# A decoder block in two parts on one core: picks moved between query columns and ahead of a wait, and the input loaded first

## The chip, the cores and the metric

One core of a Trainium2 chip runs one program. The metric is the device time of one execution in microseconds, as the median of several. The engines are TensorE (PE; its weight loads are PEld), VectorE (DVE), ScalarE (ACT), GpSimd (POOL) and SyncE (SP); DMA engines move data between HBM and the on-chip memory, issued by SP and by POOL.

## What is computed

The reference runs two blocks over one sequence of 256 tokens of 1024 numbers, in float32. The first block has two layers of band attention with a short convolution and a gated feed-forward. The second has two layers too; layer 0 has an mLSTM mixer, layer 1 stick-breaking attention over shared keys and values, and both end in an expert layer ("PEER"), cut here:

```python
def peer_ffn(h, w_q, sub_keys, peer_u, peer_v):
    def block(xb):                                    # 128 tokens
        q = einsum('td,de->te', xb, w_q).reshape(128, 8, 2, 128)
        s = einsum('thpk,pnk->thpn', q, sub_keys)     # 2 x 128 scores for each of 8 heads
        s_top, i_top = top_k(s, 16)
        ...                                           # 16 best of the 256 sums of both sides
        u = take(peer_u, expert, axis=0)              # 8 x 16 rows of 1024 for each token
        act = gelu(einsum('thkd,td->thk', u, xb))
        vv = take(peer_v, expert, axis=0)
        return einsum('thk,thkd->td', softmax(g_top) * act, vv)
```

The condition vector c passes a SiLU and a matrix product to give the shifts, scales and gates of the second block. In layer 1 of the second block q and k are normed by head before the scores.

## The kernel before, in words

The 256 tokens are two tiles of 128, with a token in each partition. An expert layer has 8 x 16 = 128 **picks** for each tile. Pick q is, for each of the tile's 128 tokens, one row of 2 x 1024 numbers (u and v of one expert) that an indirect DMA from POOL fetches into one of 10 places (`ROW`, rings `ring_b`, two slots of `wring`, `ring_c`). In the stretch from pick 248 of the whole program to pick 353 two of the 10, `ring_c`, are lent to weights, so there are 8. There are four tiles of picks: two of layer 0, then two of layer 1. The picks of one tile are worked off while the next tile's dense work runs, under one schedule written out by hand.

Each pick takes four steps. POOL (L1915) issues it once PE has released its place (`rows_free`), and, for the first of some heads, once the indices are there (`chosen`). DVE (L2672) takes the dot product of the u half with the token's row. ACT (L1709, L1713, L1719) makes gelu, weight and a diagonal matrix, for two picks at a time. PE (L1269, `weighted`) multiplies that by the v half and adds it up, two picks at a time (a pair).

How far each engine is to have come with the picks at a step of the dense work stands in `plan_of(t)` (L151): a list of step names and counts that `counted` sums up. `picks(tt, k)` on DVE does the dots up to k, `gelus(tt, k)` on ACT likewise, `weighted(tt, k)` on PE does the products up to the last whole pair before k, and with `False` up to k itself. All engines run their lists in order, so a product that isn't ready blocks what is written behind it.

`second_layer(t)` (one on each engine) is the dense work of layer 1 for tile t, with the picks of tile tt = 1 + t between its steps: norm, six weight slots ("in") for keys, values and queries, `heads_normed` of the key rows and then of the query rows on DVE (L2738), their transposes on PE (L1027, "heads"), the scores, logarithms, sums and exponents of the attention ("core", 4 groups of heads for t = 0, 8 for t = 1), output product ("o", "mid", "out"), norm ("fnorm", "fcols"), then four query column groups (`late_queries`, L1387) each followed by scores against the keys (`late_keys`, L1140), and last `choose`, the top-16 and index work on DVE, whose `choose` plan spreads picks over its own steps. `choose` of heads 0 to 3 waits for the second bank of key scores. Weights of the second layer come by SP, each into a slot that `used2` on PE returns.

At the begin SP loads the condition row `crow` (512 KB, one row to all partitions), the two halves of the input `x` (512 KB each), the 64 KB identity, small parameters and then the weights of 2 MB each, in that order (L530 on). ACT takes the SiLU of `crow` (L1434) and then the squares of `x` (L1424). PE waits for the identity, runs 28 matmul records on it (`idle_products`, L740) and then transposes the scaled input (L721). POOL waits for the first weights, loads three constants, waits for the SiLU and then loads the rows of the condition's matrix.

## Time and profile before

| | us |
|---|---|
| median of 3 runs | 2526.04 (2524.95 to 2527.66) |
| the profiled execution | 2526.39, its span 2524.7 |
| PE busy | 2032.2 (80%) |
| PE weight loads | 1384.9 (55%) |
| DVE busy | 1719.8 (68%) |
| ACT busy | 955.0 (38%) |
| POOL busy | 658.8 (26%) |
| DMA | 823.98 MB, mean 326 GB/s; indirect queue 595.97 MB |

The profile is of one execution. The page gives the busy time of each engine, the span in 40 slices (63.1 us each) and the costliest groups of instructions; the other views are the timeline (instructions in order, with the idle time before each and what ended it), the windows (busy times, clock and DMA rate of a stretch), the waits, and the DMA issues with their time to landing. A fp32 matmul has two records in it, so a pair of picks is 8 records of L1269. A product's line says "x8" for one pair. The chain of work that ended last is put down to PE by 47%, to DMA by 27% and to DVE by 11% of the span.

### The profile page before, as it was taken

The page shows a single profiled execution, that of the slowest core. Times are in us where ns is not written, and L with a number is a line of the kernel's source. Part 1 is how long each engine was busy: PE and PEld are TensorE (multiplying, and loading weights), DVE is VectorE, ACT ScalarE, POOL GpSimd, SP SyncE. Part 2 cuts the span into 40 slices and gives each one's busy share as a digit, 9 for nine tenths or more (in the row PEclk, how much of TensorE's full clock was granted, in tenths as well). Part 3 has the DMA queues.
Part 4 walks back from the last instruction along what each step waited for, and adds up shares of the span by engine and source line. Part 5 has one row for each costly group of instructions (what it writes and reads, how often), then busy time and mean ns, then how long its engine had stood idle before and what let it go on. Part 6 is the DMA issues. An engine that isn't in the chain of part 4 may idle for free.

```text
span 2524.7 us, 33890 instructions
## 1 busy us (share of the span) xinstructions
PE 2032.2 (80%) x12150; PEld 1384.9 (55%) x12150; DVE 1719.8 (68%) x3454; ACT 955.0 (38%) x2101; POOL 658.8 (26%) x631
## 2 busy tenths in 40 slices
PE   8999999999999999997665587777577778556555
PEld 7999899899989979874321123243122325211111
DVE  5687787768778867677588555558754757776544
ACT  4434533444544345432332224423223732322222
POOL 0000001000000100024445433344432335444442
PEclk9999999999999999999887798899788889887767
DMA  7545577674547763279999999999999999999998
GB/s 304 212 167 209 182 277 283 240 262 161 202 172 277 268 256 142 84 319 388 422 421 422 419 423 422 403 421 421 412 404 401 421 410 383 421 422 421 422 421 337
DMA packets 110947, 823.98 MB, mean 326 GB/s; under 512 B 14432, under 2 KB 15344, under 8 KB 31040
## 3 DMA queue, kind: packets, MB, share of 16 engines
q0 software_dynamic: 90000, 595.97, 57.8%
q1 hardware_dynamic: 20784, 225.89, 23.3%
q8 instruction: 96, 1.57, 0.2%
q14 instruction: 67, 0.55, 0.1%
HBM read 820.76 MB, written 1.05 MB: 326 GB/s over the span
## 4 chain that ended last, share of the span: by engine, by line
PE 47%; DMA 27%; DVE 11%; ACT 5%; issue 4%; POOL 2%; DVEq 2%; ACTq 1%; SPq 0%; POOLq 0%
DMA ring_b<-in_peer_uv,eidx 17%; PE pd L647 14%; PE pa L647 10%; PE pr L1269 9%; PE pr L647 7%; DMA wring<-in_peer_uv,eidx 6%; DVE wring_r L1971 2%; DVE ring_b L2672 2%; DMA ring_c<-in_peer_uv,eidx 1%; DVE wring L2672 1%; PE pa L1387 1%; ACT junk L1719 1%; POOL ring_b L1915 1%; PE pd L1292 1%; PE pa L1292 1%
## 5 line engine op out<-in xcount | busy, mean ns | idle before, releaser
L1269 PE MATMUL pr<-ring_b,junk 128*64 128x512 f32 x880 | 288.6, 765 | 156.5 <-ACT junk L1719 155.8
L1269 PE MATMUL pr<-wring,junk 128*64 128x512 f32 x840 | 269.4, 748 | 171.1 <-ACT junk L1719 170.6
L1915 POOL DMA_INDIRECT ring_b<-in_peer_uv,eidx x220 | 252.9, 1150 | 532.8 <-PE pr L1269 302.4
L2672 DVE CUSTOM_DVE_ANT_0 ring_b<-ring_b,hrow 128x1024 f32<-128x1024 f32 x220 | 267.9, 1224 | 180.9 <-DMA ring_b<-in_peer_uv,eidx 174.2
L2672 DVE CUSTOM_DVE_ANT_0 wring<-wring,hrow 128x1024 f32<-128x1024 f32 x210 | 255.4, 1223 | 187.8 <-DMA wring<-in_peer_uv,eidx 181.7
L1915 POOL DMA_INDIRECT wring<-in_peer_uv,eidx x210 | 247.8, 1180 | 332.6 <-PE pr L1269 277.3
L1709 ACT ACTIVATE gel<-dots 128x2 f32<-128x2 f32 x255 | 51.8, 203 | 654.4 <-DVE dots L2672 650.7
L1899 POOL DMA_DIRECT2D aring<-in_ada_rows x112 | 60.2, 538 | 840.9 <-DVE adal L2066 787.3
L1269 PEld LDWEIGHTS pr<-ring_b,junk 128*64 128x64 f32 x880 | 69.3, 165 | 350.8 <-ACT junk L1719 242.6
L1269 PEld LDWEIGHTS pr<-wring,junk 128*64 128x64 f32 x840 | 64.1, 159 | 345.6 <-ACT junk L1719 243.5
L1971 DVE TENSOR_TENSOR wring_r<-wring,wtop 128x2048 fp32r<-128x2048 f32 x76 | 171.7, 2261 | 54.7 <-ACT wtop L1431 52.4
L647 PE MATMUL pd<-hhi,wring_r 128*128 128x256 f32 x960 | 204.2, 281 | 0.0
L1971 DVE TENSOR_TENSOR wring_r<-wring,wring_r 128x2048 fp32r<-128x2048 f32 (+1 forms) x77 | 173.7, 2262 | 38.1 <-ACT wring_r L1431 35.7
L1431 ACT CAST wring_r<-wring 128x2048 fp32r<-128x2048 f32 x80 | 149.7, 1886 | 70.0 <-DMA wring<-in_w_mix 25.1
L1431 ACT CAST wtop<-wring 128x2048 fp32r<-128x2048 f32 x80 | 149.1, 1882 | 62.7 <-DMA wring<-in_w_back 24.4
L1269 PE MATMUL pr<-ring_c,junk 128*64 128x512 f32 x328 | 109.1, 754 | 75.1 <-ACT junk L1719 74.7
L647 PE MATMUL pa<-flo_b,wring_r 128*128 128x256 f32 x768 | 166.6, 283 | 0.0
L647 PEld LDWEIGHTS pd<-hhi,wring_r 128*128 128x128 f32 x960 | 158.6, 188 | 0.1
L1719 ACT ACTIVATE junk<-halves,gel 128x64 f32<-128x64 f32 x510 | 149.6, 340 | 17.8 <-issue 0.3
L2066 DVE CUSTOM_DVE_ANT_0 aring<-aring,crow 128x1024 f32<-128x1024 f32 x112 | 136.5, 1218 | 13.9 <-DMA aring<-in_ada_rows 12.6
L2672 DVE CUSTOM_DVE_ANT_0 ring_c<-ring_c,hrow 128x1024 f32<-128x1024 f32 x82 | 100.0, 1223 | 55.4 <-DMA ring_c<-in_peer_uv,eidx 53.5
L1713 ACT ACTIVATE gel<-gel,wexp 128x1 f32<-128x1 f32 x510 | 122.7, 287 | 18.8 <-issue 1.4
(441 smaller groups left out, 4566.4 us busy)
## 6 DMA issues: line engine op xcount, KB each, us to landing
wring<-in_w_mix SPq DMA_DIRECT2D x38, 2048.0 KB, 8.8
aring<-in_ada_rows POOLq DMA_DIRECT2D x112, 512.0 KB, 5.1
wring<-in_w_ffn SPq DMA_DIRECT2D x22, 2048.0 KB, 8.3
wring<-in_w_lstm SPq DMA_DIRECT2D x12, 2048.0 KB, 7.7
wring<-in_w_stick SPq DMA_DIRECT2D x12, 2048.0 KB, 11.7
wring<-in_w_back SPq DMA_DIRECT2D x8, 2048.0 KB, 8.1
ring_c<-in_w_stick SPq DMA_DIRECT2D x5, 2048.0 KB, 12.1
wring<-in_w_back SPq DMA_DIRECT2D x4, 1536.0 KB, 6.9
```

Of the source, the lines that this page charges most:

```text
L647: m = nc.tensor.matmul(out_, lhsT, rhs, start=start, stop=stop)
L1269: m = nc.tensor.matmul(pr[half][side, :], diag[:, p % DIAGS, :], row(p)[:, D + half * 512:D + (half + 1) * 512], start=p in FIRST_OF_SIDE, ...
L1292: i = nc.tensor.matmul(b[:, :], src(k), w(k), start=(k == 0), stop=(k == KC - 1))
L1431: nc.scalar.copy(hi, raw).then_inc(whi_ready, 1)
L1709: nc.scalar.activation(gel[:, p:p + PART], dots[:, p:p + PART], ACT.Gelu)
L1713: nc.scalar.activation(gel[:, i:i + 1], gel[:, i:i + 1], ACT.Copy, scale=wexp[:, g * PART // PICKS % NT, c // TOPK, c % TOPK:c % TOPK + 1])
L1719: nc.scalar.activation(diag[:, q % DIAGS, :], halves[:, :], ACT.Copy, scale=gel[:, q % PICKS:q % PICKS + 1]).then_inc(diag_ready, 1)
L1899: pool.dma_start(aring[:, a, :], ins["ada_rows"][bass.ds(2 * i + a, 1)].rearrange("a p n -> p (a n)")).then_inc(ada_in[a], 16)
L1915: pool.indirect_dma_start(out=row(q), out_offset=None, in_=ins["peer_uv"], in_offset=bass.IndirectOffsetOnAxis(ap=eidx[:, tt % NT, CHOSEN[ ...
L1971: nc.vector.tensor_tensor(lo, raw, hi, ALU.subtract).then_inc(wlo_ready, 1)
L2066: nc.vector.tensor_tensor_reduce(out=aring[:, j % 2, :], in0=aring[:, j % 2, :], in1=crow[:, :], scale=1.0, scalar=0.0, op0=ALU.mult, op1= ...
L2672: m = nc.vector.tensor_tensor_reduce(out=row(q)[:, 0:D], in0=row(q)[:, 0:D], in1=hrow[:, q // PICKS % NT, SIDE[q], :], scale=1.0, scalar=0 ...
```

## The change

At the begin the two loads of `x` go ahead of that of `crow` on SP, and ACT's SiLU of `crow` goes behind the squares of `x`.

In layer 1 of the second block the plan has 4 picks instead of 3 (t = 0) or 2 (t = 1) for each of the first two late query groups, 2 instead of 4 (t = 0) or 2 (t = 1) for "keys", and for t = 1 20 instead of 23 over the choice of heads. So the counts are for t = 0: "q" 74 and 78 (before 73 and 76), "keys" 80 as before; for t = 1: "q" 92 and 96 (before 90 and 92), "keys" 98 (before 94), end of the choice 118 (before 117). In the first two late query groups PE now multiplies up to two picks short of "q" after the second of the four columns, and up to "q" itself behind the group; ACT does the matching gelus ahead of its copy of the group.

DVE does the dots up to "heads" (pick 31) ahead of its wait for the query rows and their norm, where it did them up to 29 and the other two behind the norm. PE does the products up to "heads" between the transposes of the key rows and those of the query rows, and ACT does the gelus for them behind its copies of the key columns.

```diff
@@ -150,10 +150,10 @@
 
 def plan_of(t):
 
-    out, q, step = ((3, 3, 48), (2, 2, 23))[t]
+    out, q, step = ((3, 4, 48), (2, 4, 20))[t]
     return counted(0, [("first", 2), ("norm", 2), ("cols", 4), ("col0", 2), ("col1", 2)] + [(("in", j), 3) for j in range(6)]
                    + [("heads", 2)] + groups_of(t) + [("o", 2), ("mid", 4 * t), ("out0", out), ("out1", out), ("fnorm", 2), ("fcols", 2), ("fcol0", 1), ("fcol1", 1)]
-                   + [(("q", j), q) for j in range(2)] + [("keys", 4 - 2 * t)] + choice("choose", step, 2 - t))
+                   + [(("q", j), q) for j in range(2)] + [("keys", 2)] + choice("choose", step, 2 - t))
 
 
 EARLY_COLUMNS = {(0, 2): (0, 0, 2, 4), (0, 3): (8, 10, 14, 16), (1, 2): (18, 20, 20, 24), (1, 1): (28, 30, 32, 34), (1, 3): (42, 44, 46, 48)}
@@ -527,9 +527,9 @@
 
         @block.sync
         def _(sp):
-            sp.dma_start(crow[:, :], ins["c_2"].partition_broadcast(P).rearrange("p a n -> p (a n)")).then_inc(c_in, 16)
             for t in range(NT):
                 sp.dma_start(x[:, t, :], ins["x"][0, t * P:(t + 1) * P, :]).then_inc(x_in, 16)
+            sp.dma_start(crow[:, :], ins["c_2"].partition_broadcast(P).rearrange("p a n -> p (a n)")).then_inc(c_in, 16)
             sp.dma_start(ident[:, :], ins["c_ident"]).then_inc(ident_in, 16)
 
             def load(l, i):
@@ -1307,9 +1307,9 @@
                     weighted(tt, at["in", j])
                 pe.wait_ge(sqk_ready, 2 * t + 1)
                 tile_columns(bank_a, pa_full, krow)
+                weighted(tt, at["heads"], False)
                 pe.wait_ge(sqk_ready, 2 * t + 2)
                 tile_columns(bank_a, pa_full, qrow)
-                weighted(tt, at["heads"])
                 pe.wait_ge(sT_ready, t + 1)
                 pe.wait_ge(stick_in, 96)
                 groups, g0, ks = STICK_GROUPS[t], STICK_BEFORE[t], t + 1
@@ -1396,8 +1396,8 @@
                     key_bank(lambda hp, cut: qpt[:, hp, cut], j)
 
                 for j in range(2):
-                    late_queries(j)
-                    weighted(tt, at["q", j])
+                    late_queries(j, lambda c: c == 1 and weighted(tt, at["q", j] - 2, False))
+                    weighted(tt, at["q", j], False)
                     late_keys(j)
                 weighted(tt, at["keys"])
                 for j in range(2, 4):
@@ -1429,9 +1429,6 @@
             def cast_half(n):
                 raw, hi = half_of(n, wring)
                 nc.scalar.copy(hi, raw).then_inc(whi_ready, 1)
-
-            act.wait_ge(c_in, 16)
-            nc.scalar.activation(crow[:, :], crow[:, :], ACT.Silu).then_inc(c_ready, 1)
 
             na = [0]
 
@@ -1477,6 +1474,8 @@
             nc.scalar.preload_act_table_set(ROOTS)
             for t in range(NT):
                 squares(0, t)
+            act.wait_ge(c_in, 16)
+            nc.scalar.activation(crow[:, :], crow[:, :], ACT.Silu).then_inc(c_ready, 1)
             upper(0, 0)
             tile_upper(0, 0, 0)
             upper(0, 1)
@@ -1812,8 +1811,8 @@
                 for dst in (skT[:, :, cut], sqT(t)):
                     for half in range(2):
                         nc.scalar.copy(dst[:, 4 * half:4 * half + 4, :], take().rearrange("p (c n) -> p c n", n=P)).then_inc(pa_free, 1)
+                    gelus(tt, at["heads"])
                 act.drain().then_inc(sT_ready, 1)
-                gelus(tt, at["heads"])
                 groups, g0 = STICK_GROUPS[t], STICK_BEFORE[t]
 
                 def logs(i):
@@ -1859,6 +1858,7 @@
                     act.drain().then_inc(sc_ready, 1)
 
                 for j in range(2):
+                    gelus(tt, at["q", j] - 2)
                     late_query(j)
                     gelus(tt, at["q", j])
                     late_key(j)
@@ -2744,10 +2744,9 @@
                 dve.wait_ge(stick_in, 96)
                 dve.wait_ge(srow_ready, 3 * t + 1)
                 heads_normed(krow, 0, 1.0)
-                picks(tt, at["in", 5])
+                picks(tt, at["heads"])
                 dve.wait_ge(srow_ready, 3 * t + 3)
                 heads_normed(qrow, 1, SB_DIM ** -0.5)
-                picks(tt, at["heads"])
 
                 groups, g0, ks = STICK_GROUPS[t], STICK_BEFORE[t], t + 1
 
```

## Rows read from the trace of the kernel before

**Rows 1.** The page, part 2: GB/s of the DMA engines in 40 slices
```profile
GB/s 304 212 167 209 182 277 283 240 262 161 202 172 277 268 256 142 84 319 388 422 421 422 419 423 422 403 421 421 412 404 401 421 410 383 421 422 421 422 421 337
```

**Rows 2.** Issue to landing of all picks' rows, from the view by tile
```profile
DMA to landing us min/median/max: 5.6/16.3/31.0
```

**Rows 3.** Timeline of the begin: start, duration (us), engine, line, idle before
```profile
8.11 5.89 PE L740 MATMUL pa<-ident 128*128 128x128 f32 x28 [8.11 <-DMA ident<-in_c_ident]
...
13.84 1.04 PE L721 MATMUL pd<-ident,hlo 128*128 128x128 f32 x8
```

**Rows 4.** Windows of 20 us: five engines' busy us, PEclk, DMA share, GB/s
```profile
1940.00:1960.00 20.00, 14.29 (x65) 5.70 (x65) 12.75 (x22) 14.48 (x32) 11.71 (x10) 0.89 0.93 357
...
2100.00:2120.00 20.00, 17.39 (x126) 11.56 (x124) 12.47 (x53) 6.07 (x22) 9.19 (x10) 1.00 0.76 304
```

**Rows 5.** Timeline of tile C's late queries, PE, POOL and DVE
```profile
2087.42 7.41 PE L1387 MATMUL pa<-hT,ring_c 128*128 128x128 f32 x64 [0.82 <-DVEq L2394]
...
2105.20 1.94 PE L1269 MATMUL pr<-wring,junk 128*64 128x512 f32 x8
...
2108.53 0.94 POOL L1915 DMA_INDIRECT wring<-in_peer_uv,eidx  x1 [8.37 <-issue]
...
2091.91 1.23 DVE L2672 CUSTOM_DVE_ANT_0 wring<-wring,hrow 128x1024 f32<-128x1024 f32 x1 [1.28 <-DMA wring<-in_peer_uv,eidx]
...
2108.70 1.65 DVE L2577 MAX8 top<-sc 128x8 f32<-128x128 f32 x8 [5.63 <-ACTq L1859]
...
2166.73 0.23 DVE L2654 TENSOR_TENSOR eidx<-hilof 128x64 int32<-128x64 f32 x1
...
2178.99 0.94 POOL L1915 DMA_INDIRECT ring_c<-in_peer_uv,eidx  x1 [0.31 <-issue]
```

**Rows 6.** Timeline of tile C's query rows, all engines
```profile
1910.90 1.55 POOL L1915 DMA_INDIRECT ring_b<-in_peer_uv,eidx  x1 [0.30 <-issue]
...
1926.82 1.22 DVE L2404 TENSOR_TENSOR cand<-sc 128x1024 f32<-128x1024 f32 x1
...
1935.02 1.97 PE L1027 MATMUL pa<-ident,sc 128*128 128x128 f32 x8 [10.18 <-DVEq L2738]
...
1936.92 2.70 PE L1269 MATMUL pr<-ring_b,junk 128*64 128x512 f32 x8
...
1937.02 0.58 ACT L1814 COPY hT<-pa 128x512 f32<-128x512 f32 x1 [0.27 <-PE pa L1027]
...
1939.55 1.71 PE L1325 MATMUL pd<-hT,skT 64*128 64x128 f32 x16
...
1945.51 5.24 PE L1269 MATMUL pr<-wring,junk 128*64 128x512 f32 x16 [2.38 <-ACT junk L1719]
...
1949.84 0.94 POOL L1915 DMA_INDIRECT wring<-in_peer_uv,eidx  x1 [2.94 <-PE pr L1269]
```

**Rows 7.** DMA issues, us to landing: tile C's pick 31, then 68
```profile
ring_b<-in_peer_uv,eidx POOLq DMA_INDIRECT x1, 22.8
...
ring_b<-in_peer_uv,eidx POOLq DMA_INDIRECT x1, 6.7
```

**Rows 8.** Waits of DVE in tile C's core, 1960 to 2028 (us, times, longest)
```profile
DVE sc L2773 <- PE pr L1338: 15.4, 7, 3.2
...
DVE wring L2672 <- DMA wring<-in_peer_uv,eidx: 0.3, 1, 0.3
```

**Rows 9.** Waits of DVE in tile B's core, 1575 to 1616
```profile
DVE wring L2672 <- DMA wring<-in_peer_uv,eidx: 5.0, 4, 1.3
```

**Rows 10.** Timeline of tile B's query rows, POOL and DVE
```profile
1520.68 0.93 POOL L1915 DMA_INDIRECT ring_c<-in_peer_uv,eidx  x1 [0.30 <-issue]
...
1540.49 1.22 DVE L2404 TENSOR_TENSOR cand<-sc 128x1024 f32<-128x1024 f32 x1
```

**Rows 11.** DMA issues, us to landing: tile B's pick 31, then 42
```profile
ring_c<-in_peer_uv,eidx POOLq DMA_INDIRECT x1, 28.5
...
wring<-in_peer_uv,eidx POOLq DMA_INDIRECT x1, 13.5
```

## The prediction

> **What bounds the kernel now.** I read the page first. Over the first 17 slices (to 1073 us) the DMA rate swings between 84 and 304 GB/s; from the 20th on it stands at 421 to 424 in most slices [rows 1]. That is the part in which the picks of the expert layers are fetched. A pick is one row of 8 KB for each of 128 tokens, 1.05 MB, so at 422 GB/s a pick costs 2.48 us, and what is left of the span is a count of megabytes plus the stretches in which the DMA engines had nothing to do. The change moves no byte, so after the first layers only those stretches count. The windows of 20 us show the two that matter here: 1940 to 1960 at 357 GB/s, which is (422 - 357) / 422 x 20 = 3.1 us lost, and 2100 to 2120 at 304, which is 5.6 us [rows 4]. A stretch is lost when all places of the ring are landed and not yet multiplied, so that POOL can't issue. The next question is therefore always the same: when does PE multiply pair (q, q+1), since POOL issues the pick 8 places on (10 in most stretches) right behind it. An issue needs at least 5.6 us to land; the median is 16.3 [rows 2], and the difference is what a late product may cost for nothing.
>
> I call the second layer's two token tiles B and C, and count picks from 0 in each.
>
> **The begin.** PE starts at 8.11, when the identity lands, and runs 28 products on it for 5.89 us; the first transpose of the input starts at 13.84, behind them [rows 3]. The identity is issued behind both the input and the condition row, in either order, so 8.11 stays. The input may land 1.2 us sooner (512 KB at 422 GB/s) and waits longer for PE. ACT's SiLU of the condition row moves behind the squares of the input, and GpSimd, which waits for it before its first weight rows, has a wait for the first weights ahead of that one. Price 0, bounds -0.3 and +0.3. The cover is the 5.89 us of products on the identity.
>
> **Tile C's query rows.** Before, DVE ends the dot of pick 29 at 1926.82 and at once norms the query rows, until 1935.02, when PE transposes them [rows 6]: 8.2 us. Now the dots of picks 30 and 31 come first. Pick 31 is issued at 1910.90 [rows 6] and lands 22.8 us later [rows 7], at 1933.7; the DMA engines are saturated until then, so it can't land sooner. Its dot ends at 1933.7 + 1.2 = 1934.9, the norm at 1943.1, so the query rows are 8.1 us later. That is an added wait: behind it on DVE stand the norm and the dots of 32 and 33, and PE, ACT and the whole core wait for the norm.
> What is gained: pair (28, 29) was multiplied at 1936.92, behind the transposes, and goes now right behind the key columns, at 1928, so picks 36 and 37 are issued 9 us sooner and the stall at 1940 goes. It also stood in the way of the first scores: ACT had the columns ready at 1937.02 + 0.58, PE began the scores at 1939.55 [rows 6]. So 8.1 - 1.9 = 6.2 us is the delay of the core; ACT's table loads and logarithms follow the scores at a fixed distance, and the products of 32 to 35, which began at 1945.51 and released the issue at 1949.84 [rows 6], move to 1951.7 and 1956.0.
> Pick 31 lands at 1933.7 and the queue is now never empty, so pick 39 lands 8 x 2.48 us later, at 1953.6. Pick 40 lands at 1956.0 + 5.6 = 1961.6. So the stall is not removed, it is moved 12 us on and is longer.
> Is it given back in the core? In tile C's core DVE waits 15.4 us for PE's sums and 0.3 us for rows [rows 8]: the chain scores, logarithms, sums, exponent, gelus sets the pace there and keeps a delay. The ring has 8 places here, and pick 68 landed 6.7 us after its issue [rows 7], 1.1 above the least. So of 6.2 us of delay 1.1 is free and 5.1 reach the DMA engines; since a restart leaves its second pick late too, I take +5.3. Bounds: +6.4 if nothing is free, and -3.1 if the core catches up and only the old stall goes. I take the upper part because the core's own waits [rows 8] are for PE, nearer to it than the landing waits that a catch-up needs.
>
> The Trainium skill (DMA: Bandwidth & Descriptors, Anatomy of one DMA) puts a transfer from GpSimd's queue at about 2.0 us plus its bytes at 436 GB/s, an estimate of 4.4 us for a lone pick. The trace has 5.6 as its least [rows 2], and it decides; by 4.4 the term would be 1.2 us less, +4.1.
>
> **Tile B's query rows.** The same step: pick 31 lands at 1520.68 + 28.5 = 1549.2, its dot ends at 1550.4, and the norm that began at 1540.49 [rows 10, 11] begins 9.9 us later; with 2 us given back as above the core is 7.9 us late. But there are 10 places here: pick 42, the first that waits for a core product, took 13.5 us to land [rows 11], 7.9 above the least. Just enough. And in this core DVE waits 5.0 us for rows on one ring alone [rows 9], so the delay shrinks by the core's end. I take +0.5, bounds 0 and +1.5.
>
> **The late queries.** In tile B the change only moves products inside the same ten picks; DVE does the dots up to pick 79 before its choice of heads, before and after, and the 27th slice (1641 to 1704 us) that holds the step stands at 421 GB/s [rows 1], with no stall to win: 0, bounds -0.5 and +0.5. In tile C the first 64 matmuls of a query column group start at 2087.42 and last 7.41 us; pair (88, 89) was multiplied at 2105.20, behind two groups, and POOL could issue pick 96 only at 2108.53 [rows 5]. That is the 5.6 us stall. Now pair (86, 87) goes at 2091 in the middle of the first group and (88, 89) behind it at 2094.7 (the dot of 89 begins at 2091.91 [rows 5] and ends 1.2 later, plus 1.5 us on ACT). Pick 96 is issued at 2097.4, pick 98 at 2101 (the place returns when the group is done, 5.4 us later than before, still early), 100 at 2105, 102 at 2112, 104 at 2119.5. With pick 89 landed at 2091.9 and 2.48 us for each, 104 must be issued by 2091.9 + 37.2 - 5.6 = 2123.5. The stall goes: -5.6.
> What is late next: five pairs instead of two lie ahead of the second key bank, and two waits for ACT, so the choice of heads, which began at 2108.70, begins at 2120.6. DVE has 20 picks to do in it instead of 23; from 2108.70 to the indices at 2166.73 [rows 5] it took 58.0 us, so at most 58.0 - 3 x 1.2 = 54.4 now, until 2175.0. Pick 0 of the next tile was issued at 2178.99 [rows 5] and lands by the median at 2195.3; with everything 5.6 us sooner it must be issued by 2195.3 - 5.6 - 5.6 = 2184. Covered by 9 us. But pick 98, landed at 2091.9 + 9 x 2.48 = 2114.2, gets its dot at 2122: DVE is 8 us behind the landings, and the margins of the issues shrink to a few us (104: 4). I add +0.5; bounds of the whole term -5.6 and -2.6.
>
> **Sum.** 0 + 0.5 + 5.3 - 5.6 + 0.5 = +0.7 us. The profiled execution took 2526.39 (span 2524.7 and 1.7 around it), 0.35 above the median of the runs, 2526.04; on the median the sum gives 2526.7, which I round to 2527.
>
> **Rivals.** (1) The query rows cost nothing: the core of tile C catches up and both stalls go, -3.1 - 5.6 + 0.5 + 0.5 = -7.7, 2518. For it: the delay starts with four more picks landed. Against it: DVE's waits in that core [rows 8]. It decides if the core's pair period is below two times 4 picks' landing, 19.8 us. Chance 0.24. (2) The late gain fails, slower: the choice of heads begins 12 us later and DVE, 8 us behind the landings, frees places too late, so that the stall at 2104 comes back inside the choice. It decides when the choice ends later than 2184, or an issue comes later than 5.6 us before its landing's turn. Price: the query term stays alone, +0.5 + 5.3 + 0.5, with 0.5 to 2 of new gaps: 2533. Chance 0.17. (3) The moves cancel nothing and do nothing, since all picks wait in the ring anyway: 2526. Against it: the two stalls of [rows 4] lie exactly on the moved steps. Chance 0.04. The forecast has 0.55.
>
> **How the numbers follow.** The forecast's own range is 2522.5 to 2531.5 (query term 3 to 6.4, late term -5.6 to -2.6, tile B 0 to 1.5). The whole range, 2517.5 to 2532, takes in rival 1 and stops short of most of rival 2. A measurement of this kernel can tell about 0.2% (5 us) from no change. Faster by that is rival 1 with a little of the forecast's edge, 0.25; slower is rival 2 with a little, 0.18; the rest, 0.57.
>
> **What would show it.** In the changed kernel's trace: the first 14 us as before; tile C's query transposes near 1943 (+ what tile B added) instead of 1935.02; a stall not at 1940 but near 1954 to 1960, and issue-to-landing times in tile C's core near 6; no stall at 2104, with products between the columns of each late group; the choice of heads starting near 2121. Wrong if the query transposes move by under 5 us, if the windows from 1940 to 2040 hold more than 415 GB/s on average, or if a new stall stands between 2120 and 2200.

## The result, and the profile after

| | median us (runs) | ratio to the kernel before | profiled execution |
|---|---|---|---|
| before | 2525.83 (6) | | 2526.39, span 2524.7 |
| after | 2536.95 (6) | 1.0046 [1.0033, 1.0059] | span 2534.8 |

The change costs 11 us. The forecast was 2527.0, range 2517.5 to 2532, with 0.57 on no change that can be told and 0.18 on slower: the measured time lies 5 us above the range. A ratio of 0.001 is 2.5 us here; below, each ratio is turned into us with 2526.

The DMA rates of the page after, to be held against [rows 1]: the 25th, 31st and 35th slice fell (422 to 390, 401 to 372, 422 to 371), and the 34th, with the old stall at 2104, rose (383 to 408). The view has one figure for each slice of 63 us.

```profile
GB/s 303 211 167 208 190 271 284 240 254 167 202 169 286 265 247 161 87 320 385 422 421 422 419 424 390 408 422 421 421 416 372 414 397 408 371 423 421 422 421 354
```

Windows of 20 us of the kernel after, with the columns of [rows 4]. The stall at 2100 is gone (304 to 422 GB/s). The one at 1940 is deeper (357 to 268), and there are new ones in tile B's core behind the query rows (1560), in tile C's choice (2140) and at its end (2180). The first fence has the kernel before for these three windows, the second the kernel after.

```profile
1560.00:1580.00 20.00, 16.93 (x56) 6.21 (x54) 14.66 (x25) 14.45 (x31) 10.32 (x9) 0.76 1.01 419
...
2140.00:2160.00 20.00, 11.71 (x80) 6.82 (x80) 16.97 (x43) 8.26 (x22) 9.68 (x8) 0.92 1.01 420
...
2180.00:2200.00 20.00, 10.57 (x32) 2.29 (x32) 10.86 (x18) 5.19 (x21) 9.03 (x8) 0.83 1.01 421
```

```profile
1560.00:1580.00 20.00, 14.09 (x54) 6.50 (x52) 12.01 (x22) 13.71 (x27) 4.41 (x6) 0.66 0.82 324
1940.00:1960.00 20.00, 12.56 (x52) 7.25 (x51) 12.01 (x21) 13.60 (x27) 4.82 (x5) 0.60 0.67 268
2100.00:2120.00 20.00, 15.98 (x107) 10.74 (x106) 9.86 (x16) 4.99 (x17) 9.82 (x9) 0.91 1.02 422
2140.00:2160.00 20.00, 14.72 (x108) 9.88 (x108) 19.49 (x76) 6.35 (x23) 12.15 (x8) 1.00 0.98 383
2180.00:2200.00 20.00, 14.71 (x96) 6.69 (x98) 11.51 (x22) 10.27 (x34) 6.15 (x6) 0.74 0.83 321
```

The timeline of tile C's query rows, answering to [rows 6]: DVE starts the norm at 1935.09 behind the dot of pick 31 (before 1926.82), PE transposes the query rows at 1943.30 (1935.02), begins the scores at 1945.98 (1939.55) and the core's first pairs at 1952.85 (1945.51). POOL, idle for 13.11 us, issues pick 40 at 1957.13 (1949.84).

```profile
1935.09 1.22 DVE L2404 TENSOR_TENSOR cand<-sc 128x1024 f32<-128x1024 f32 x1
...
1943.30 1.97 PE L1027 MATMUL pa<-ident,sc 128*128 128x128 f32 x8 [2.95 <-DVEq L2738]
1945.98 3.09 PE L1325 MATMUL pd<-hT,skT 64*128 64x128 f32 x16 [0.71 <-ACTq L1815]
1952.85 5.19 PE L1269 MATMUL pr<-wring,junk 128*64 128x512 f32 x16 [3.78 <-ACT junk L1718]
...
1957.13 0.94 POOL L1915 DMA_INDIRECT wring<-in_peer_uv,eidx  x1 [13.11 <-PE pr L1269]
```

The timeline of tile C's late queries and the end of its choice, answering to [rows 5], with ACT's lines (ACT's line numbers are one lower in the kernel after): products stand between the column halves (2100.24), pick 96 is issued at 2107.34, and then DVE sits idle for 9.07 us (before 5.63) until the second key bank, and starts the choice at 2131.47. At the end ACT waits 6.68, 4.60 and 5.70 us for PE's fourth query group, fourth key bank and the 64 matmuls of the rows, and POOL waits 7.12 and 5.82 us for products.

```profile
2100.24 1.94 PE L1269 MATMUL pr<-ring_b,junk 128*64 128x512 f32 x8
...
2107.34 0.94 POOL L1915 DMA_INDIRECT wring<-in_peer_uv,eidx  x1 [1.53 <-issue]
...
2131.47 0.68 DVE L2577 MAX8 top<-sc 128x8 f32<-128x128 f32 x3 [9.07 <-ACTq L1858]
...
2171.58 0.58 ACT L1853 COPY cand<-pa 128x512 f32<-128x512 f32 x1 [6.68 <-PE pa L1387]
2178.29 0.58 ACT L1857 COPY sc<-pa 128x512 f32<-128x512 f32 x1 [4.60 <-PE pa L1140]
2178.97 1.28 ACT L1682 ACT_TABLE_LOAD   x1
2180.26 0.26 ACT L1682 ACTIVATE wexp<-wexp 128x64 f32<-128x64 f32 x1
2190.23 0.58 ACT L1677 COPY hrow<-pa 128x512 f32<-128x512 f32 x1 [5.70 <-PE pa L1130]
...
2187.78 1.65 POOL L1915 DMA_INDIRECT ring_b<-in_peer_uv,eidx  x1 [7.12 <-PE pr L1269]
...
2199.26 1.22 POOL L1915 DMA_INDIRECT ring_c<-in_peer_uv,eidx  x1 [5.82 <-PE pr L1269]
```

Where the time went, by comparing the landing of the same pick in both traces (after less before): +0.7 when tile B begins, +3.5 at its pick 52, +1.5 at tile C's pick 34, +5.9 at 52, +8.1 at 84, +3.3 at 102, +11.7 at the next tile's pick 0, and +10.7 to +12.6 from there. So there are three steps: tile B's query rows, tile C's query rows, and a gain of 5 us between picks 84 and 102 that is more than given back before the tile ends.

### The profile page after: what moved, and what is told of

Same layout as the page of the kernel before. It is cut to its first block, busy times and chain, and to the rows that moved or that the text cites. A ratio compares the mean times of both kernels' runs of the same rounds, so it can differ in the third digit from the quotient of the medians.

```text
span 2534.8 us, 33890 instructions
## 1 busy us (share of the span) xinstructions
PE 2051.4 (81%) x12150; PEld 1393.1 (55%) x12150; DVE 1717.7 (68%) x3454; ACT 954.8 (38%) x2101; POOL 649.5 (26%) x631
## 4 chain that ended last, share of the span: by engine, by line
PE 48%; DMA 24%; DVE 13%; ACT 6%; issue 4%; POOL 2%; DVEq 2%; ACTq 1%; SPq 0%; POOLq 0%
PE pd L647 14%; DMA ring_b<-in_peer_uv,eidx 12%; PE pr L1269 10%; PE pa L647 10%; DMA wring<-in_peer_uv,eidx 7%; PE pr L647 5%; DMA ring_c<-in_peer_uv,eidx 3%; PE pa L1292 3%; DVE wring_r L1971 2%; DVE ring_b L2672 2%; DVE wring L2672 2%; ACT junk L1718 1%; PE pd L1292 1%; POOL ring_b L1915 1%; DMA aring<-in_ada_rows 1%
## 5 line engine op out<-in xcount | busy, mean ns | idle before, releaser
L1269 PE MATMUL pr<-wring,junk 128*64 128x512 f32 x840 | 274.6, 760 | 151.2 <-ACT junk L1718 150.9
L1915 POOL DMA_INDIRECT wring<-in_peer_uv,eidx x210 | 239.1, 1138 | 338.1 <-PE pr L1269 293.2
L1269 PE MATMUL pr<-ring_c,junk 128*64 128x512 f32 x328 | 121.5, 837 | 86.3 <-ACT junk L1718 86.2
L2066 DVE CUSTOM_DVE_ANT_0 aring<-aring,crow 128x1024 f32<-128x1024 f32 x112 | 136.5, 1219 | 12.2 <-DMA aring<-in_ada_rows 11.0
L1915 POOL DMA_INDIRECT ring_c<-in_peer_uv,eidx x82 | 94.7, 1155 | 142.5 <-PE pr L1269 120.9
```

The costliest lines, as they stand in the source:

```text
L1269: m = nc.tensor.matmul(pr[half][side, :], diag[:, p % DIAGS, :], row(p)[:, D + half * 512:D + (half + 1) * 512], start=p in FIRST_OF_SIDE, ...
L1915: pool.indirect_dma_start(out=row(q), out_offset=None, in_=ins["peer_uv"], in_offset=bass.IndirectOffsetOnAxis(ap=eidx[:, tt % NT, CHOSEN[ ...
L2066: nc.vector.tensor_tensor_reduce(out=aring[:, j % 2, :], in0=aring[:, j % 2, :], in1=crow[:, :], scale=1.0, scalar=0.0, op0=ALU.mult, op1= ...
```

## The experiments

Every kernel is the kernel before with the edit shown, unless it says otherwise. The times are ratios to the kernel before, measured beside it, with 95% intervals. The diffs are cut to the lines that matter.

**Which part costs.** First the begin alone: the two `x` loads ahead of `crow`, and the SiLU behind the squares.

```diff
-            sp.dma_start(crow[:, :], ...)
             for t in range(NT):
                 sp.dma_start(x[:, t, :], ...)
+            sp.dma_start(crow[:, :], ...)
```

> Only the begin of the change on the kernel before: the input is loaded ahead of the condition row, and ACT takes the SiLU behind the squares. Theory: nothing, 0 +- 0.5 us, with the first products on the identity at 7.9 to 8.1 us and the first transpose of the input at 13.8 to 13.9. Rival: the condition row and GpSimd's first weight rows come later and the first layer keeps the 0.75 us that the changed kernel had lost before the second layer began: +0.7 to +1 us, seen in the landing of tile B's pick 0.

Measured: 1.0009 [1.0000, 1.0018], +2.3 us (0 to +4.5). The kernel after has the first products at 7.90 and the first transpose at 13.93 ([rows 3]: 8.11 and 13.84); this kernel's own trace has 8.24 and 13.34. The lines are of the kernel after:

```profile
7.90 6.19 PE L740 MATMUL pa<-ident 128*128 128x128 f32 x28 [7.90 <-DMA ident<-in_c_ident]
13.93 1.04 PE L721 MATMUL pd<-ident,hlo 128*128 128x128 f32 x8
```

Tile B's first picks come 2.5 us late in the trace of this run, but 3.6 and 3.8 us late in two other traces below whose begin is that of before, so no mechanism can be read from it; from tile C's pick 40 on it is 0.2 us late. Whether the begin costs 1 to 2 us stays open; a gain is excluded.

The query rows' part alone, in both tiles, in tile C, and in tile B:

```diff
                 tile_columns(bank_a, pa_full, krow)
+                weighted(tt, at["heads"], False)
                 pe.wait_ge(sqk_ready, 2 * t + 2)
                 tile_columns(bank_a, pa_full, qrow)
-                weighted(tt, at["heads"])
...
-                picks(tt, at["in", 5])
+                picks(tt, at["heads"])
                 dve.wait_ge(srow_ready, 3 * t + 3)
                 heads_normed(qrow, 1, SB_DIM ** -0.5)
-                picks(tt, at["heads"])
```

> Only the query rows' part, in both tiles: the dots, gelus and products of picks 30 and 31 ahead of the norm of the query rows. Theory A (the core's chain is rigid, and what the norm waits for pick 31 stays to the end): tile B's core 8 us later, of which 2.3 to 3 us reach the DMA engines; tile C +5.5 by its pick 52 and +1 to +1.5 more behind the core; the choice of heads starts that much later and gives nothing back; the whole is +8 to +9 us (2534.5). Theory B (the two parts cost so much only together, since each takes from the same reserve of the choice): heads alone +5.5 to +6, tile C's term being eaten in part by the stall at 2104 that is still there.

Measured: 1.0054 [1.0041, 1.0067], +13.6 us (10.4 to 16.9), above what both theories expected. Its trace, again one execution, ends 6.8 us late.

> The query rows' part in tile C alone. Theory A: tile B as before; in tile C +5.3 to +5.5 us by pick 52, +6.5 at the end of the tile: 2532.5. My forecast's own term was +5.3. Theory of a catch-up (rival 1 of the forecast): -3 us. The difference to the run with both tiles gives tile B's term: 2.3 to 3 us by theory A, 0.5 by the forecast.

Measured: 1.0038 [1.0025, 1.0051], +9.6 us (6.3 to 12.9). Its trace has tile C's query transposes at 1942.23 and +5.7 us from there to the end; the profiled execution, 2531.74, is the fastest of five.

> The query rows' part in tile B alone. The forecast's term: +0.5 us. By the traces of the runs with both tiles, +3.3 us on the landings by its pick 52, of which some is taken up again by tile C's pick 40: +1 to +3. By the difference of the medians: +4.

Measured: 1.0004 [0.9995, 1.0013], +1.0 us (-1.3 to +3.3).

The late queries' part alone:

```diff
-    out, q, step = ((3, 3, 48), (2, 2, 23))[t]
+    out, q, step = ((3, 4, 48), (2, 4, 20))[t]
...
-                    late_queries(j)
-                    weighted(tt, at["q", j])
+                    late_queries(j, lambda c: c == 1 and weighted(tt, at["q", j] - 2, False))
+                    weighted(tt, at["q", j], False)
```

> Only the late queries and the plan's numbers for them (10 picks between the queries and the choice's 20 in tile C). Theory A (the choice and what ACT and PE do around the fourth key bank are a chain of their own, which starts some 3.5 us later and frees the places of picks 116 to 118 late): the stall at 2104 goes, -5.6 us at pick 98, and comes back behind pick 107, above all at picks 124 and 125; the net is +1 to +3.5 us (2528.5). Theory B (the give-back of 8 us is an interaction with the core's delay): without that delay the gain stays in good part, -3 to -5 us (2522).

Measured: 1.0006 [0.9997, 1.0015], +1.5 us. Here is the whole story without any delay from the core. By the landings it is at +0.1 us at pick 84, -5.9 at 98, -4.1 at 120, and +1.5 at the next tile's pick 0: 6 us won, 7.4 given back. The give-back needs no query rows' part, so theory B falls. Half of it is at one place: pick 124 lands 6.16 us behind pick 123, where 2.48 is the pace. DVE's idle time ahead of the choice and the windows of this kernel:

```profile
2121.92 1.65 DVE L2578 MAX8 top<-sc 128x8 f32<-128x128 f32 x8 [9.06 <-ACTq L1859]
...
2100.00:2120.00 20.00, 15.61 (x106) 10.71 (x106) 6.56 (x12) 5.57 (x18) 6.68 (x6) 0.91 1.01 421
2140.00:2160.00 20.00, 17.58 (x119) 10.53 (x115) 18.96 (x65) 6.14 (x22) 10.94 (x9) 1.00 0.99 388
2160.00:2180.00 20.00, 12.75 (x68) 6.18 (x68) 18.62 (x31) 7.69 (x20) 6.73 (x5) 0.74 0.87 362
2180.00:2200.00 20.00, 13.68 (x98) 5.76 (x94) 7.18 (x13) 8.37 (x29) 12.75 (x11) 0.91 0.95 363
```

The changed kernel again, measured beside some of its parts:

> The changed kernel itself, on the chip of these runs. +11 us, as measured. If the parts add up (begin +1, query rows +12, late queries +1.4) it is +14; if the late queries win inside the changed kernel, +9.

Measured: 1.0047 [1.0034, 1.0061], +11.9 us. The parts give 2.3 + 1.0 + 9.6 + 1.5 = 14.4, each with 2 to 3 us of uncertainty, so they add up within it. With the 13.6 of the query rows' part in both tiles, in place of the 1.0 and 9.6, they give 17.4, which is less close.

**Why the query rows' part costs.** DVE's edit alone (the last four lines of the diff above), with PE and ACT as before:

> Only VectorE's part of the query rows' edit, in both tiles: the dots of picks 30 and 31 ahead of the norm, with TensorE's products and ScalarE's gelus where they were. If the norm's wait for pick 31 is the whole price, as the forecast has it: the same as the whole part, +8 to +12 us (2535), and 1 to 2 us more than that in tile C, since pair (28, 29) stays behind the norm. If the order on TensorE and ScalarE costs, 0 to +3.

Measured: 1.0061 [1.0047, 1.0074], +15.4 us (11.9 to 18.7), against 13.6 for the whole part: within the uncertainty, two dots ahead of the norm and DVE's waits for their rows are the whole price. (In the kernel after DVE is idle for 2.50 us until pick 30 lands and for 3.72 us until pick 31 does.) DVE starts the norm at 1937.17, PE the transposes at 1945.37, and the window at 1940 falls to 202 GB/s.

```profile
1937.17 1.22 DVE L2404 TENSOR_TENSOR cand<-sc 128x1024 f32<-128x1024 f32 x1
...
1945.37 1.97 PE L1027 MATMUL pa<-ident,sc 128*128 128x128 f32 x8 [13.98 <-DVEq L2738]
...
1940.00:1960.00 20.00, 12.26 (x50) 5.42 (x52) 12.33 (x27) 11.20 (x25) 3.75 (x4) 0.67 0.52 202
```

The other half, PE's product of pair (28, 29) between the transposes, with DVE's order as before:

```diff
                 tile_columns(bank_a, pa_full, krow)
+                weighted(tt, at["in", 5], False)
                 pe.wait_ge(sqk_ready, 2 * t + 2)
```

> The kernel before with one edit on TensorE alone: the pair (28, 29), whose dots and gelus are done, is multiplied between the key and the query columns; DVE norms the query rows behind the dot of pick 29, as before. Theory (the old stall at 1940 to 1960 is the late product of 28 and 29, and what the changed kernel pays is the norm's wait for pick 31): the stall goes, -3.1 us, and the core starts 1.9 us sooner, so -3 to -5 us by tile C's pick 52, and all of it kept: 2521.5. Rival: the stall only moves on to the first core products (picks 40 and 41), since they are released at the same time: 0 to -1 us.

Measured: 0.9998 [0.9989, 1.0007], -0.5 us (-2.8 to +1.8). The window at 1940 is full and no time is won that could be measured:

```profile
1940.00:1960.00 20.00, 13.57 (x59) 5.52 (x57) 13.79 (x24) 14.77 (x34) 7.79 (x7) 0.88 1.01 420
2100.00:2120.00 20.00, 18.13 (x133) 12.49 (x134) 11.19 (x44) 5.54 (x18) 9.63 (x9) 1.00 0.77 291
```

PE transposes the query rows at 1936.93, 1.9 us later than before, in an execution whose picks are 3.6 us late here, and it starts the scores at 1938.81 (before 1939.55) and the next groups at 1951.89 (1950.67). Counted from the transposes, the scores start 2.65 us sooner and the next groups only 0.7. The matmuls of the scores (x16) take 3.09 us instead of 1.71 here. So most of the gain is lost again inside the core. The 3.1 us that I read as lost in [rows 4] were not won. They also belong to one execution: in five other traces whose code in this stretch is that of before (the late part, its two variants, the numbers alone and the placed pairs) this window has 392 to 409 GB/s, not 357.

**Why the late part gives its gain back.** First suspect: with "keys" at 98, the fourth key bank and the copy of the rows stand four picks further on. On the late part alone I put them back in tile C:

```diff
-                    late_queries(j, lambda c: weighted(tt, at["keys"] + LATE_COLUMNS[j][c], False))
+                    late_queries(j, lambda c: weighted(tt, at["keys"] - 4 * t + LATE_COLUMNS[j][c], False))
...
-                weighted(tt, at["keys"] + LATE_ROWS_BACK, False)
+                weighted(tt, at["keys"] - 4 * t + LATE_ROWS_BACK, False)
```

> The late queries' part alone, as in the run of that name, with one size put back: in tile C the fourth key bank and the copy of the rows stand behind the same picks as in the kernel before (110 and 114), not four picks further on (114 and 118). Theory A1 (ACT's wait for the fourth queries and keys and TensorE's 64 matmuls of the rows, four picks late, hold the products of 116 to 119, and so picks 124 and on): the gaps at 124 and 125 go and 4 to 5.5 of the 7.4 us given back stay won: the next tile's pick 0 lands 3 to 5 us sooner than in the kernel before, 2522. Theory A2 (the choice itself starts too late and would free the places too late wherever these stand): the gaps at 124 and at the next tile's pick 0 stay, +0 to +1.5.

Measured: 0.9999 [0.9988, 1.0010], -0.3 us against +1.5 for the late part. The window from 2180 still has 383 GB/s.

> The changed kernel with the fourth key bank and the copy of the rows of tile C back behind picks 110 and 114. By theory A1 it gets 4 to 5 us back and stands at +6 to +7 over the kernel before (2532.5), which is the price of the query rows' part alone. By theory A2 it stays at +10 to +11 (2536.5).

Measured: 1.0038 [1.0025, 1.0051], +9.6 us against +11.6. In both the edit is worth 2 us, within the uncertainty, and not the 4 to 5.5 expected: at most a small part.

Second suspect: the choice's start. The plan's numbers alone, no product moved into a group:

```diff
-    out, q, step = ((3, 3, 48), (2, 2, 23))[t]
+    out, q, step = ((3, 4, 48), (2, 4, 20))[t]
...
-                   + [(("q", j), q) for j in range(2)] + [("keys", 4 - 2 * t)] + choice("choose", step, 2 - t))
+                   + [(("q", j), q) for j in range(2)] + [("keys", 2)] + choice("choose", step, 2 - t))
```

> The plan's numbers of the change alone (98 picks ahead of tile C's choice instead of 94, 20 in it instead of 23), with the products where they were, behind whole groups. By A2 and A3 the choice starts 3 to 9 us later with the stall at 2104 still there: slower, +3 to +8 us (2531), lost between pick 98 and the next tile's pick 0. If the choice's start is not what counts, 0 +- 1.

Measured: 0.9991 [0.9982, 1.0000], -2.3 us, against what both theories expected. The numbers alone put pair (88, 89) behind the first group (2097.14) instead of behind the second (2105.20), which is all that the stall at 2104 needed: the window from 2100 has 415 GB/s. And DVE, with four more dots to do, is not idle ahead of the choice:

```profile
2097.14 1.94 PE L1269 MATMUL pr<-wring,junk 128*64 128x512 f32 x8 [0.15 <-ACT junk L1719]
...
2112.61 1.27 DVE L2672 CUSTOM_DVE_ANT_0 wring<-wring,hrow 128x1024 f32<-128x1024 f32 x1 [1.21 <-DMA wring<-in_peer_uv,eidx]
...
2113.81 1.64 DVE L2577 MAX8 top<-sc 128x8 f32<-128x128 f32 x8
```

So a choice that begins 5.1 us later costs nothing here, with DVE at work until it begins. What differs in the late part is DVE's idle time, and the later start that comes with it. Ahead of each key bank of the late part stands a pair behind the whole group, (90, 91) and (94, 95), and PE waits 2.19 us for each. In the late part alone:

```profile
2102.32 2.79 PE L1269 MATMUL pr<-wring,junk 128*64 128x512 f32 x8 [2.19 <-ACT junk L1719]
2104.89 1.92 PE L1140 MATMUL pa<-keysT,cand 128*64 128x128 f32 x16
...
2116.25 0.59 ACT L1854 COPY cand<-pa 128x512 f32<-128x512 f32 x1 [7.29 <-PE pa L1387]
2116.95 0.20 ACT L1709 ACTIVATE gel<-dots 128x2 f32<-128x2 f32 x1
...
2118.41 1.94 PE L1269 MATMUL pr<-ring_b,junk 128*64 128x512 f32 x8 [2.19 <-ACT junk L1719]
2120.18 1.04 PE L1140 MATMUL pa<-keysT,cand 128*64 128x128 f32 x16
```

It isn't a wait for rows: pick 95 had landed at 2106.60 and its dot was done at 2107.85. ACT's gelus of the pair are written behind its copy of the group, and ACT stood idle for 7.29 us ahead of that copy. No run puts these gelus ahead of the copy. I took the `False` off the call behind the group and left the rest of the late part:

```diff
                     late_queries(j, lambda c: c == 1 and weighted(tt, at["q", j] - 2, False))
-                    weighted(tt, at["q", j], False)
+                    weighted(tt, at["q", j])
```

> The late queries' part alone, with pairs between the columns as in the change, but the pair behind a whole group is the one that the kernel before would take: the pair (94, 95) is multiplied behind the second key bank, not ahead of it. Theory A4 (the fifth pair ahead of the key bank, which waits for picks 94 and 95 to land and for their dots and gelus, delays the bank and the choice by 6 to 8 us, and that is what gives the gain back): the key bank near 2112 and the choice near 2114, as in the run with the numbers alone, and with it -3 to -5 us (2522). Rival (the halves of the query groups themselves cost, by TensorE's waits between them): still +0 to +2.

Measured: 0.9986 [0.9977, 0.9995], -3.5 us, and no overlap with the late part's own interval. The edit does more than I wrote down ahead of it: it moves two pairs of tile C. Pair (94, 95) goes behind the second key bank, and pair (90, 91), which stood behind the first group, goes into the middle of the second, so the first key bank is 2.6 us sooner and the second, at 2115.24 (2120.18 in the late part alone), 4.9. In tile B two pairs move likewise. DVE's idle time is 2.92 us instead of 9.06, and the windows at 2140 and 2160 are full again or nearly so:

```profile
2102.32 1.09 PE L1140 MATMUL pa<-keysT,cand 128*64 128x128 f32 x16 [0.71 <-ACTq L1855]
...
2107.11 1.94 PE L1269 MATMUL pr<-wring,junk 128*64 128x512 f32 x8
...
2115.24 1.09 PE L1140 MATMUL pa<-keysT,cand 128*64 128x128 f32 x16 [0.71 <-ACTq L1855]
...
2117.21 1.65 DVE L2578 MAX8 top<-sc 128x8 f32<-128x128 f32 x8 [2.92 <-ACTq L1859]
...
2140.00:2160.00 20.00, 16.91 (x114) 10.59 (x116) 18.93 (x57) 6.73 (x24) 10.27 (x9) 0.99 1.01 421
2160.00:2180.00 20.00, 13.50 (x104) 6.58 (x100) 14.63 (x26) 7.44 (x17) 6.34 (x6) 0.75 1.01 412
2180.00:2200.00 20.00, 10.95 (x46) 3.48 (x48) 10.67 (x20) 7.83 (x32) 11.07 (x10) 0.93 0.99 391
```

Shown by this is the place of the two pairs behind the groups; how much each is worth is open. That it acts through DVE's idle time is my reading of the traces and not shown. A rival stands: the choice may start as late as 2117 for nothing (8.5 us later than before) and not as late as 2121.92, whatever DVE does ahead of it, and these kernels can't tell the two apart, since their dots end within 1.5 us of each other. The measured gains don't order themselves by idle time either: -2.3 with 0 us and -3.5 with 2.92, which is the same within the uncertainty.

The same edit in the changed kernel:

> The changed kernel with the same one pair behind the second key bank. If the parts add up, it gets back what e13_late_whole got against e3_late, 6.4 us: +5 us over the kernel before (2531). If in the changed kernel the choice is late anyway through the core, 0 to 2 us of it: +9 to +11.

Measured: 1.0025 [1.0014, 1.0036], +6.3 us (3.5 to 9.1) against +11.9 (8.6 to 15.4): 5.6 us come back. One argument of one call is about half of what the change costs.

An inconclusive one: the plan as before, and pairs (86, 87) and (88, 89) in the middle of the two groups.

```diff
-                    late_queries(j)
+                    late_queries(j, lambda c: c == 1 and weighted(tt, t and at["q", j] - 2, False))
```

> On the kernel before, tile C's pairs (86, 87) and (88, 89) are multiplied in the middle of the first and of the second late query group, with the plan's numbers as before: the same two pairs stand ahead of the second key bank, so the choice starts no later. Theory A2 (what gives the gain back is the choice's late start, by three more pairs and their waits ahead of the second key bank): pick 96 is issued near 2102 instead of 2108.5, the stall at 2100 to 2120 loses 3 to 5 us, and it stays won: 2522. Rival A3 (the choice of heads and the work around it is a chain that sets the next tile's start wherever its rows land; the stall at 2104 is slack of that chain): the window from 2100 fills up and the gain is given back by the next tile's pick 0 just the same: 0 +- 1 us.

Measured: 1.0000 [0.9991, 1.0010]. It did not do what I built it for: pair (88, 89) went at 2103.9, only 1.3 us sooner, and pick 96 was issued at 2107.2, not 2102; the window at 2100 has 343 GB/s. DVE's idle time rose to 8.36 us. So it doesn't speak on A3; the two kernels above do, since both keep what they win past the next tile's pick 0. But it bears on the rival named above. Its choice starts 3.6 us later than before, sooner than in both of them, with more idle time ahead of it:

```profile
2112.28 1.65 DVE L2577 MAX8 top<-sc 128x8 f32<-128x128 f32 x8 [8.36 <-ACTq L1859]
```

From pick 102 to the next tile's pick 0 it gives back 3.3 us; the numbers alone, with a start 5.1 us later and no idle time, give back 0.9. That speaks for the idle time and against the start, in one trace each and with different counts of picks in the choice.

**Versions that win.** The pair (28, 29) between the transposes, on top of four of these kernels. On the placed pairs:

> The same placing with the pair (28, 29) between key and query columns as well. Both stalls that the profile of before shows in tile C are thereby attacked with no dot ahead of a norm and no later choice. By my forecast's own counting of stalls: -7 to -8 us (2518). If the chains of the core and of the choice set the time, and not the stalls of the DMA engines: 0 to -1.5 us.

Measured: 0.9994 [0.9983, 1.0005]. On the late part with key bank and rows put back:

> Both edits together on the kernel before. If each wins what its theory says and they add up: -7 to -9 us, 2518. If the second stall was only fed by the first (less delay ahead of it leaves the same end): the larger of the two alone, -4 to -5.

Measured: 0.9995 [0.9986, 1.0004]. On the plan's numbers alone:

> The plan's numbers alone and the pair (28, 29) between key and query columns: the two edits that won or cost nothing. If they add up: -4 to -5.5 us against the kernel before (2521). If the pair adds nothing, as alone: -3.7.

Measured: 0.9985 [0.9976, 0.9994], -3.8 us. And on the late part without the `False`:

> The late queries' part with the pair (94, 95) behind the second key bank, and the pair (28, 29) between the key and the query columns, on the kernel before; the begin as before. The first alone measured -5.0 us, the second alone 0 to -1.8: -5 to -6.5 us together (2520.5).

Measured: 0.9981 [0.9972, 0.9990], -4.8 us. This one beats both kernels, by 4.8 and by 16 us. The pair (28, 29) shows 0.5 to 1.5 us in its favour in each of the five comparisons with and without it, never more than their uncertainty.

## Why the prediction was wrong, step by step

**The begin, forecast 0.** The cover held: in both traces the first transpose of the input stands behind the products on the identity, and it starts at 13.93 and 13.34 (before 13.84) because these take 6.19 and 5.26 us (5.89). No gain came of it. The size is 0 to +4.5 us; the bound of +0.3 may have been too narrow.

**Tile B's query rows, forecast +0.5.** Alone +1.0 (-1.3 to +3.3): inside the bounds. The reasoning was too kind, though. I let the core be 7.9 us late against 7.9 us of slack; in the kernel after the landings fall 2.8 us further behind by pick 52. What saved the sum is that 2 us of it are taken up again ahead of tile C's core, which I had not counted on. That also happens to other delays: in the kernels with the numbers alone and with the placed pairs, tile C's pick 34 landed 3.1 us late and pick 40 only 1.4 and 0.9.

**Tile C's query rows, forecast +5.3 (-3.1 to +6.4).** The path was right. Transposes were to be near 1943 and came at 1943.30, pick 40 was to be issued at 1956.0 and was at 1957.13, the stall moved instead of going, and the core kept the delay: from pick 40 to pick 64 the dots are 6.6 to 7.0 us late, and four of them 8.6. The run with DVE's edit alone shows the cause. The size, +9.6 us (6.3 to 12.9), is at or over my upper bound. The trace accounts for 5.7 us; what the other executions of the same kernel lose beyond it stays open. The sum took 1.9 us of credit for the pair (28, 29) out of the scores' way, and not all of it lasted: the transposes come 8.3 us later, the scores 6.4, but the core's first pairs 7.3, since the matmuls of the scores take 3.09 us instead of 1.71, with the granted clock at 0.50 from 1944 to 1953. My bound of -3.1 and my first rival rested on the old stall: filled by the pair alone, it returned nothing that could be measured.

**The late queries, forecast -5.6 + 0.5.** This is the step that failed: alone it measured +1.5 (-0.8 to +3.8), 6.6 us of the miss of 10.9. The first half was right: pick 98 lands 5.9 us sooner, the choice was to begin at 2120.6 and began at 2121.92, the indices were to be there by 2175.0 and were at 2170.48. What was wrong is the last +0.5, and the sentence "Covered by 9 us" that it leans on: in the trace 7.4 us are given back, not 0.5. I checked the margin of the indices, and that of the places only up to pick 104. From my own numbers DVE had its dot of pick 97 done at about 2113 and the choice at 2120.6, some 8 us of idle time against 5.63 in the kernel before, and I counted only its work (three dots fewer) and not that gap. It was 9.06 us. DVE comes out of it with rows landed and not dotted. Pair (114, 115), which frees the place of pick 124, is multiplied 2.9 us later than in the kernel before and takes 3.68 us instead of 1.94, so POOL issues pick 124 at 2178.22 instead of 2173.58; pair (118, 119), which frees that of the next tile's pick 0, is 9.6 us later, and that issue 8.9. From the idle time to these products the path is not traced through: the dots of picks 115 to 118 are by then only 1.3 to 3.0 us later than before, and ACT and PE, with their fourth query group, key bank and rows, stand between. That is my second rival, which I gave 0.17 and priced at 2533. Of its two conditions the first (indices later than 2184) did not hold, the second did: the turn of pick 124 was at 2181.2, so its issue was due at 2175.6.

I also credited the wrong edit. The stall at 2104 goes with the plan's numbers alone; the products between the columns add nothing to it that the runs show, and the `False` behind the group costs 5 us (+1.5 against -3.5).

**The signs I named.** "Wrong if a new stall stands between 2120 and 2200" came true: 383 GB/s from 2140 and 321 from 2180. The other two did not, and both concern the part that was right.

**The least time of a pick.** In the kernel after the shortest time from issue to landing is 5.4 us (pick 40 of tile C, issued behind 13.11 us in which POOL had nothing to issue), against 5.6 in [rows 2]. The Trainium skill (DMA: Bandwidth & Descriptors, Anatomy of one DMA) gives an estimate of 4.4 us for it; the trace has 1.0 us more, and it decides.

## What to carry to other kernels

When work is moved ahead of a wait, price the idle time that it puts on the engine behind the wait, not only the work: here two pairs ahead of two key banks, each 2.19 us behind its gelus, made the difference between -3.5 and +1.5 us, and VectorE idled for 9.06 us instead of 2.92; that the idle time is the link is likely, not shown. Don't let the first instruction of a serial chain wait for a transfer that comes later than its own input; the norm of the query rows did, for pick 31, and of 8 us the chain kept 6 to 7. And a window in which the DMA engines idle is only worth its microseconds if the chain behind it gets on sooner: one edit that filled the window won 0.5 us (-2.8 to +1.8).

## What the runs showed of the hardware

The product of one pair takes PE 1.94 us in half of its 256 places, where the granted clock is 1.00 (the upper of its two levels, 2.4 GHz), and 3.68 us where it is 0.50 (1.2 GHz), behind idle time of the engine. In the kernel after the window from 1940 has a granted clock of 0.60 (before 0.89), and the stretch from 2183 to 2187 has 0.50. First a line of the kernel before, with 1.00 from 2175 to 2178, then two of the kernel after:

```profile
2175.64 1.94 PE L1269 MATMUL pr<-ring_c,junk 128*64 128x512 f32 x8 [1.13 <-ACT junk L1719]
```

```profile
2183.29 3.68 PE L1269 MATMUL pr<-ring_b,junk 128*64 128x512 f32 x8 [5.05 <-ACT junk L1718]
2194.83 3.63 PE L1269 MATMUL pr<-ring_c,junk 128*64 128x512 f32 x8 [1.99 <-ACT junk L1718]
```

A switch of ACT's table costs 1.28 us: the load at 2178.97 is followed by the exponent at 2180.26, 0.01 us behind its end (lines above). The Trainium skill (ScalarE: Activation LUTs, What ACT_TABLE_LOAD costs) adds a drain to it, about 2.66 us in all; this trace shows no room for it, with 0.10 us ahead of the load and 0.01 behind.

The first part of the program varies from execution to execution by as much as the whole change costs: the dot of tile B's first pick comes between 0.2 us (the query rows' part alone) and 12.2 us (the fastest kernel, the last of the versions that win) later than in the kernel before, with the same instructions ahead of it. Only differences within a stage of a trace, and ratios of several runs, were of use.
